# Modulations between the quarters of a panel's own weights, the norm's weight in column factors, and layer 1's transposes and gate rows inside its attention

## The chip, the cores and the metric

One Trainium2 chip, one core. The metric is the device time of one execution in microseconds; the shown value is the median of several runs. The trace comes from one more execution under the profiler.

## What is computed

A two-layer block and then one layer of a second block, all float32, 256 tokens of 2048 columns. Cut to what matters here:

```python
# first block; adaLN vectors come from one row c times a wide matrix
for l in range(2):
    mod = silu(c) @ w_mod[l] + b_mod[l]              # 2048 x 6144
    shift, scale, gate = split(mod, 3)
    h = x * (1 + scale) + shift
    y = diff_attention(h, ...) if l == 0 else forgetting_attention(h, w_q, w_out, k, v, F)
    # layer 1: k, v, F from shared_kv(x, silu(c) @ w_mod_kv + b_mod_kv, ...)
    x = layer_norm(sqrt(2) * x + gate * y, ln_g[l], ln_b[l])
# forgetting attention: o = softmax(q k' + F[t] - F[s]) v * silu(g);  return o @ w_out
# second block: S5 mixer, GLU, squared-relu MLP, with its own modulation (2048 x 12288)
```

Between the layers stands `x = layer_norm(...)` (weight `ln_g[0]`, bias `ln_b[0]`), which feeds three things: layer 1's `h` (modulated), the keys' and values' `h` (modulated by another vector) and the residual.

## The kernel before, in words

All five engines have a program written out by hand, in one order each; two planners (`tables`, a ring of six 1 MB slots for weights and a set of PSUM banks) only count who uses which slot and which bank in which turn, so the order in `tables` must be that of every engine.

The front's matrices are taken in 24 **steps** (`FRONT`): four panels of 512 columns each of layer 0's output projection (steps 0 to 3), layer 1's q (4 to 7), g (8 to 11), k (12 to 15), v (16 to 19) and its output projection (20 to 23). A panel's weights come in four quarters of 1 MB, each a slot of the ring. float32 products are made of three products of split operands: ScalarE makes the high part of each half quarter (`w_hi`), VectorE the low part (`w_lo`), and TensorE (`multiply`) runs 96 products of 512 columns, or 192 of 256, over eight half quarters. ScalarE's `w_hi(h)` waits until half h-4 has been multiplied.

A **modulation** is 512 columns of one of the wide matrices, 4 MB, also four quarters of the ring. There are 56 (`MODS`): 20 to 27 give layer 1's shift and scale, 28 to 35 those of keys and values, 36 to 39 layer 1's gate, 40 and on the second block's. TensorE multiplies one into bank 4 (`mod`: 16 products 128x32 by 512 columns, four side by side in four column groups of the array), ScalarE copies the bank to `ROWS`, and TensorE sums four row groups into columns (`sums`, which waits for that copy). `sums(j-1)` is called at the head of `mod(j)`. Twelve modulations (`DVE_MOD`) are multiplied by VectorE, in pieces between its splits (`mod_piece`), and their quarters come in the ring between those of two panels (`DVE_PART`).

Where TensorE's modulations stand before: 23 to 25 inside layer 0's attention (`MOD_AT_A`, at t = 5, 9, 13 of 21), 26 to 28 after steps 0 to 2, 29 while the layer norm is made (`MOD_AT_LN`), 30 to 37 after steps 4 to 11 (`MOD_AT_STEP`), 41 to 46 inside layer 1's attention (`MOD_AT_B`, t = 2, 7, ..., 27 of 35). VectorE's 38, 39, 40 stand in steps 12 to 17. Each is loaded as a whole, behind the panel that it follows. SP issues the loads, in the order of the ring, and blocks at a slot until what it holds has been used.

Layer 0's attention (lines 2440 to 2469 of TensorE's program) is a loop of 21 turns over 16 score blocks, software-pipelined: scores, VectorE's bias and maximum, ScalarE's exponentials, VectorE's mix, transpose, product with v. Before it, SP reloads the projections from DRAM (`proj_d`, lines 686 to 697): q and k, then v behind the last block's end, then the gate; POOL writes the S5 state to DRAM (line 879), and VectorE and ScalarE start the attention when it has landed, since they use its buffer.

After step 3 comes `layer_norm(0)`: statistics, then for each of two row tiles (x - mean) * weight and * rstd + bias, each in two halves; TensorE transposes the result (`turn_in`), and ScalarE and VectorE apply the modulation's factor and shift per column and split it (`split_in`). The same x is transposed again before step 12, and POOL stores it in DRAM.

Layer 1's attention (lines 2504 to 2532) is the same kind of loop, 35 turns over 32 blocks of 128 or 256 columns. Behind it stand `to_T(1)`, the transposes of the attended heads with their split, the broadcast of the gate over the partitions (`bcast("m1g")`, into the place of half of q) and the first splits of step 20's weights.

Of the kernel before, what the change touches and what calls it, by code (L numbers as in the profile page):

```python
# [117 lines left out]
def tables():  # L118
# [12 lines left out]
    def step(n):  # L131
        for q in range(4):
            if (n, q) in DVE_PART:
                ring.use(("mod", *DVE_PART[n, q]), slots)
            ring.use(("step", n, q), slots)
        for b in range(2):
            bank.use(("step", n, b), GD)

# [44 lines left out]
    for t in range(21):  # L183
# [6 lines left out]
        if t in MOD_AT_A:  # L190
            mod(MOD_AT_A[t])
        if t >= 17:
            bank.use(("bc", "m0g", t - 17), GC)
    for layer in range(2):
        for k in range(8):
            bank.use(("oT", layer, k), (GO, GA)[layer])
        if layer:
            for q in range(4):
                bank.use(("bc", "m1g", q), GC)
        for n in (range(0, N_W1), range(N_W1, N_GLU))[layer]:  # L200
# [6 lines left out]
            if n in MOD_AT_STEP:  # L207
                mod(MOD_AT_STEP[n])
# [7 lines left out]
        for t in range(35):  # L216
# [6 lines left out]
            if t in MOD_AT_B:  # L223
                mod(MOD_AT_B[t])
    bank.use(("ss", 1), GC)
# [24 lines left out]
def build(nc, A, out):  # L250
    ctx = ExitStack()
    with ctx:
# [8 lines left out]
                 "pcol", "xn", "xres", "xsq", "ysq", "ones", "dtaken", "dmod"]  # L261
# [84 lines left out]
        def chunk_lo(*key):  # L346
# [15 lines left out]
                ("mpost", A["norm_mlp_post_2"].rearrange("l (r n) -> (l r) n", n=128), 16)]  # L362
# [33 lines left out]
        def mod_acc(j):  # L396
            at = MSB if j > 47 else L2
            return at[:, 512 * (DVE_NO[j] % 2):512 * (DVE_NO[j] % 2) + 512]
# [89 lines left out]
        bcA, lnG, lnB = reg(24576, 2048), reg(26624, 2048), MSB[:, :]  # L488
        res_tmp = sm[:, 0:512]
# [145 lines left out]
        def sync_program(sp):  # L635
# [18 lines left out]
            def load_w(key, W, k0, n0):  # L654
                for q in range(4):
# [3 lines left out]
                    load(key, W, k0, n0, q)  # L659

# [36 lines left out]
            sp.dma_start(reg(4096, 4096), proj_d[3]).then_inc(S["p3"], 16)  # L697
# [3 lines left out]
            for t in sorted(MOD_AT_A):  # L701
                mod(MOD_AT_A[t])

# [13 lines left out]
            for n in range(N_W1):  # L717
                step(n)
                if n in MOD_AT_STEP:
                    mod(MOD_AT_STEP[n])  # L720
# [67 lines left out]
        def gpsimd_program(g):  # L788
# [94 lines left out]
            def norm_rows(l):  # L883
# [4 lines left out]
                g.dma_start(lnG, A["ln_g"][l:l + 1, :].to_broadcast([128, 2048])).then_inc(S["bcg"], 16)  # L888
# [17 lines left out]
        def scalar_program(a):  # L906
# [37 lines left out]
            def to_T(layer):  # L944

                for k2 in range(8):
# [238 lines left out]
            for t in range(21):  # L1185
# [16 lines left out]
                if t in MOD_AT_A:  # L1202
                    mod(MOD_AT_A[t])
# [7 lines left out]
            for n in range(N_W1):  # L1211
                if n == N_Q:
# [3 lines left out]
                    split_in("q", h_raw["q"], sc1, M("m1", 0), 2, AHk, 8 * n)  # L1216
# [131 lines left out]
        def vector_program(v):  # L1348
# [76 lines left out]
            def round_of(n, last=False):  # L1425
                for h in range(8 * n + 4, 8 * n + (8 if last else 12)):
# [6 lines left out]
                    w_lo(h)  # L1433
                    if n < 8 and h % 2:
# [3 lines left out]
                if last:  # L1438
                    finish(n)

# [497 lines left out]
            def layer_norm(l):  # L1938
# [7 lines left out]
                v.wait_ge(S["bcg"], 16 * (l + 1))  # L1946
                v.wait_ge(S["bcb"], 16 * (l + 1))
# [9 lines left out]
            for n in range(N_W1):  # L1957
                if n == N_Q - 1:
                    mod_bias("m1s")
                if n == N_Q:  # L1960
                    layer_norm(0)
                    own()
                    ts(sc1, M("m1", 16), 1.0, None, ADD, None, *o.up("scol"))
                    split_in("q", h_raw["q"], sc1, M("m1", 0), AHk, ALk, N_Q, 8 * n)
# [679 lines left out]
```

## Time and profile before

| | us |
|---|---|
| median of 3 runs | 2741.72 |
| lowest and highest | 2737.67, 2751.97 |
| profiled execution, its own time | 2757.5 |
| its span | 2755.6 |

Busy of the span: TensorE's products 2501.9 (91%), its weight loads 2059.6, VectorE 1714.8 (62%), ScalarE 1041.8 (38%), GpSimd 177.4. TensorE's granted clock was 0.925 of 2.4 GHz on average: it has two levels, 1.2 and 2.4 GHz, so 0.50 in a stretch is the lower and 1.00 the higher. The DMA engines read 646.77 MB.

How to read it: times in rows are from the span's start. A row of a timeline names the engine, the line, the operation, what is written and read, and in brackets the idle time before it with what ended it. "x8" are eight records; a float32 product leaves two.

### The profile page before, as it was taken

The page shows a single profiled execution, that of the slowest core. Times are in us where ns is not written, and L with a number is a line of the kernel's source. Part 1 is how long each engine was busy: PE and PEld are TensorE (multiplying, and loading weights), DVE is VectorE, ACT ScalarE, POOL GpSimd, SP SyncE. Part 2 cuts the span into 40 slices and gives each one's busy share as a digit, 9 for nine tenths or more (in the row PEclk, how much of TensorE's full clock was granted, in tenths as well). Part 3 has the DMA queues.
Part 4 walks back from the last instruction along what each step waited for, and adds up shares of the span by engine and source line. Part 5 has one row for each costly group of instructions (what it writes and reads, how often), then busy time and mean ns, then how long its engine had stood idle before and what let it go on. Part 6 is the DMA issues. An engine that isn't in the chain of part 4 may idle for free.

```text
span 2755.6 us, 42740 instructions
## 1 busy us (share of the span) xinstructions
PE 2501.9 (91%) x18111; PEld 2059.6 (75%) x18111; DVE 1714.8 (62%) x2630; ACT 1041.8 (38%) x1556; POOL 177.4 (6%) x289
## 2 busy tenths in 40 slices
PE   5799999798789799989998958899899999999998
PEld 1588877566656598789854848578699898998986
DVE  4657789688767755356524755777755477655555
ACT  0253343344453333344423322344444444343443
POOL 1102233011100000111000000000000000000000
PEclk7799999899899899989977975999999999999999
DMA  9969999787678688969766748868645587755553
GB/s 353 337 219 356 349 336 313 234 294 288 244 260 308 244 286 308 353 209 312 258 220 218 249 90 309 327 232 276 236 133 189 183 274 276 244 184 191 188 171 107
DMA packets 317373, 699.74 MB, mean 254 GB/s; under 512 B 13600, under 2 KB 14080, under 8 KB 312192
## 3 DMA queue, kind: packets, MB, share of 16 engines
q1 hardware_dynamic: 298432, 627.27, 66.2%
q0 software_dynamic: 18480, 67.66, 7.0%
q8 instruction: 143, 2.34, 0.3%
q10 hardware_dynamic: 272, 2.10, 0.2%
q14 instruction: 46, 0.38, 0.0%
HBM read 646.77 MB, written 56.49 MB: 255 GB/s over the span
## 4 chain that ended last, share of the span: by engine, by line
PE 73%; DVE 15%; DMA 8%; ACT 2%; issue 1%; SPq 0%; POOL 0%; DVEq 0%; ACTq 0%; POOLq 0%
PE bank L2147 71%; DVE arena L1352 5%; DMA ring<-in_w_mod 3%; DMA ring<-in_a_w_in 3%; DVE ring_lo L1352 3%; DVE sm L1352 2%; DVE arena L1360 2%; PE bank L2150 1%; PE bank L2375 1%; DMA ring<-in_a_w_out 1%; DMA arena<-arena 0%; DVE MSB L1352 0%; DMA m_state<-MSB 0%; DVE LT L1360 0%; ACT att_w_hi L963 0%
## 5 line engine op out<-in xcount | busy, mean ns | idle before, releaser
L1352 DVE TENSOR_TENSOR ring_lo<-ring,w_hi 128x1024 fp32r<-128x1024 f32 (+1 forms) x380 | 427.7, 1134 | 359.9 <-ACT w_hi L963 334.8
L963 ACT CAST w_hi<-ring 128x1024 fp32r<-128x1024 f32 x316 | 330.6, 1049 | 472.5 <-PE bank L2147 470.4
L1352 DVE TENSOR_TENSOR ring_lo<-ring,att_w_hi 128x1024 fp32r<-128x1024 f32 x192 | 232.0, 1223 | 224.1 <-ACT att_w_hi L963 223.9
L963 ACT CAST att_w_hi<-ring 128x1024 fp32r<-128x1024 f32 x192 | 198.9, 1049 | 350.8 <-PE bank L2147 181.0
L2147 PE MATMUL bank<-in_hi,w_hi 128*128 128x256 f32 x1024 | 290.2, 283 | 1.2 <-DVE n L1357 1.2
L2147 PE MATMUL bank<-in_lo,w_hi 128*128 128x256 f32 x1024 | 290.1, 283 | 0.0
L2147 PE MATMUL bank<-in_hi,ring_lo 128*128 128x256 f32 x1024 | 289.7, 283 | 0.0
L2147 PE MATMUL bank<-w_hi,hid_lo 128*128 128x512 f32 x640 | 257.5, 402 | 5.2 <-DVE ring_lo L1352 5.2
L2147 PE MATMUL bank<-ring,cpad 128*32 128x512 f32 x1408 | 195.7, 691 | 26.1 <-DMA ring<-in_w_mod 22.5
L2147 PE MATMUL bank<-att_w_hi,att_hi 128*128 128x512 f32 x512 | 206.0, 402 | 6.9 <-DVE ring_lo L1352 6.9
L2147 PE MATMUL bank<-ring_lo,att_hi 128*128 128x512 f32 x512 | 202.7, 396 | 0.0
L2147 PE MATMUL bank<-w_hi,hid_hi 128*128 128x512 f32 x512 | 202.6, 396 | 0.0
L2147 PE MATMUL bank<-att_w_hi,att_lo 128*128 128x512 f32 x512 | 202.0, 395 | 0.0
L2147 PE MATMUL bank<-ring_lo,hid_hi 128*128 128x512 f32 x512 | 201.5, 394 | 0.0
L913 ACT CAST in_lo<-ring 128x512 fp32r<-128x512 f32 x192 | 115.6, 623 | 213.9 <-PE bank L2147 107.7
L2147 PEld LDWEIGHTS bank<-in_hi,w_hi 128*128 128x128 f32 x1024 | 195.2, 191 | 1.4 <-DVE n L1357 1.3
L2147 PEld LDWEIGHTS bank<-in_hi,ring_lo 128*128 128x128 f32 x1024 | 194.9, 190 | 0.0
L2147 PEld LDWEIGHTS bank<-in_lo,w_hi 128*128 128x128 f32 x1024 | 194.4, 190 | 0.1
L1352 DVE TENSOR_TENSOR ring_lo<-ring,in_lo 128x512 fp32r<-128x512 f32 x192 | 129.5, 702 | 72.2 <-ACT in_lo L913 72.2
L2147 PE MATMUL bank<-hid_lo,in_lo 128*128 128x256 f32 (+1 forms) x528 | 156.1, 296 | 16.2 <-DVE ring_lo L1352 16.2
L2147 PE MATMUL bank<-w_hi,in_hi 128*128 128x512 f32 x368 | 148.6, 404 | 3.3 <-DVE ring_lo L1352 3.3
L2147 PE MATMUL bank<-att_hi,att_w_hi 128*128 128x256 f32 x512 | 146.6, 286 | 2.3 <-issue 2.3
(259 smaller groups left out, 4998.5 us busy)
## 6 DMA issues: line engine op xcount, KB each, us to landing
ring<-in_w_mod SPq DMA_DIRECT2D x192, 1024.0 KB, 9.5
ring<-in_a_w_in SPq DMA_DIRECT2D x64, 1024.0 KB, 10.2
ring<-in_w_mlp_in SPq DMA_DIRECT2D x64, 1024.0 KB, 5.2
ring<-in_w_mlp_out SPq DMA_DIRECT2D x64, 1024.0 KB, 5.1
ring<-in_kv_w_mod SPq DMA_DIRECT2D x32, 1024.0 KB, 10.7
ring<-in_b_w_in SPq DMA_DIRECT2D x32, 1024.0 KB, 6.9
ring<-in_kv_w SPq DMA_DIRECT2D x32, 1024.0 KB, 5.6
ring<-in_s_w_glu SPq DMA_DIRECT2D x32, 1024.0 KB, 5.5
```

Of the source, the lines that this page charges most:

```text
L913: return a.copy(dst, src).then_inc(*(to or o.up("act")))
L963: a.copy(whi(h), raw_half(h)).then_inc(*o.up("whi"))
L1352: return v.tensor_tensor(dst, x, y, op).then_inc(*(to or o.up("dve")))
L1360: return v.scalar_tensor_tensor(out=dst, in0=x, scalar=s1, in1=y, op0=o1, op1=o2).then_inc(*(to or o.up("dve")))
L2147: return p.matmul(dst, l_, r_, start=start, stop=stop, skip_group_check=True)
L2150: return p.transpose(dst, src, ident[0:k, 0:k])
L2375: t = p.transpose(bank("u", run, pc)[:, 32 * j:32 * j + 32], HT[run][at, e, j, :, :].rearrange("p q h -> p (q h)"), ident[at, at])
```

## The change

It keeps the work of modulations and moves it: 23 to 26 go into steps 0 to 3 and 29 to 36 into steps 4 to 11, with each quarter loaded and multiplied behind two half quarters of the panel; 27 and 28 stand at the layer norm; none stands in layer 0's attention; 37 goes to VectorE (steps 12 and 13), with 38 to 40 two steps later each, and the last quarter of 40 in the first turns of layer 1's attention. `sums(j-1)` of these modulations is called at the head of `multiply`. The load of the gate projection (proj 3) is issued behind the wait for the S5 state. `layer_norm(0)` makes only (x - mean) * rstd; the modulation's factor and shift take in the norm's weight and bias as columns, and x itself is given its weight and bias in 16 pieces in steps 4 and 5. In layer 1's attention the modulations stand at t = 5, 10, ..., 30, seven of eight transposes at t = 8, 12, ..., 32, the gate's broadcast at t = 18, 22, 26, 30 and the first splits of step 20 at t = 31 to 34.

```diff
-MOD_AT_A = {5: 23, 9: 24, 13: 25}
-MOD_AT_STEP = {0: 26, 1: 27, 2: 28, **{n: 26 + n for n in range(4, 12)}}
-MOD_AT_LN = (29,)
-MOD_AT_B = {2 + 5 * i: 41 + i for i in range(6)}
+MOD_AT_STEP = {**{n: 23 + n for n in range(4)}, **{n: 25 + n for n in range(4, 12)}}
+MOD_AT_LN = (27, 28)
+MOD_AT_B = {5 + 5 * i: 41 + i for i in range(6)}
+TURN_AT_B = {4 * k + 8: k for k in range(7)}
+GATE_AT = {18 + 4 * q: q for q in range(4)}
...
-DVE_MOD = {38: 12, 39: 14, 40: 16, 47: 20, 48: 24, 49: 26, 50: 28, 51: 30, 52: 40, 53: 42, 54: 44, 55: 46}
+DVE_MOD = {37: 12, 38: 14, 39: 16, 40: 18, 47: 20, 48: 24, 49: 26, 50: 28, 51: 30, 52: 40, 53: 42, 54: 44, 55: 46}
...
-SUMS_AT = {12: 37, 14: 38, 16: 39, 18: 40, 20: 46, 22: 47, 26: 48, 28: 49, 30: 50, 31: 51, 42: 52, 44: 53, 46: 54, 48: 55}
+SUMS_AT = {12: 36, 14: 37, 16: 38, 18: 39, 20: 46, 22: 47, 26: 48, 28: 49, 30: 50, 31: 51, 42: 52, 44: 53, 46: 54, 48: 55}
+DVE_PART[N_W1 - 1, 3] = DVE_PART.pop((N_W1, 0))
...
@@ build: vecs, the row copies
-                ("mpost", A["norm_mlp_post_2"].rearrange("l (r n) -> (l r) n", n=128), 16)]
+                ("mpost", A["norm_mlp_post_2"].rearrange("l (r n) -> (l r) n", n=128), 16),
+                ("lng", A["ln_g"][0:1].rearrange("l (r n) -> (l r) n", n=128), 16),
+                ("lnb", A["ln_b"][0:1].rearrange("l (r n) -> (l r) n", n=128), 16)]
+        lnG0 = [L2[:, 512 * i:512 * i + 512] for i in range(3)] + [L1[:, 1536:2048]]
+        q_shift = st[:, 176:192]
...
@@ sync_program, load_w
                     load(key, W, k0, n0, q)
+                    if key[0] == "step" and key[1] in MOD_AT_STEP:
+                        j = MOD_AT_STEP[key[1]]
+                        load(("mod", j), MOD_W[MODS[j][0]], 0, 128 * MODS[j][1], q)
...
             sp.wait_ge(S["blm"], 32)
-            sp.dma_start(reg(4096, 4096), proj_d[3]).then_inc(S["p3"], 16)
             sp.wait_ge(S["ms0"], 16 * 16)
             sp.wait_ge(S["ms1"], 16 * 16)
-            for t in sorted(MOD_AT_A):
-                mod(MOD_AT_A[t])
+            sp.dma_start(reg(4096, 4096), proj_d[3]).then_inc(S["p3"], 16)
             for n in range(N_W1):
                 step(n)
-                if n in MOD_AT_STEP:
-                    mod(MOD_AT_STEP[n])
...
@@ scalar_program (the same inserts stand in vector_program, with w_lo)
-                    split_in("q", h_raw["q"], sc1, M("m1", 0), 2, AHk, 8 * n)
+                    split_in("q", h_raw["q"], sc1, q_shift, 2, AHk, 8 * n)
                 if t in MOD_AT_B:
                     mod(MOD_AT_B[t])
-            for h in range(8 * N_W1, 8 * N_W1 + 4):
-                w_hi(h)
-            to_T(1)
-            bcast("m1g", bcA)
+                if t - 1 in GATE_AT:
+                    bcast("m1g", bcA, GATE_AT[t - 1])
+                if t - 1 in TURN_AT_B:
+                    to_T(1, TURN_AT_B[t - 1])
+                if t > 30:
+                    w_hi(8 * N_W1 + t - 31)
+            to_T(1, 7)
...
@@ vector_program
+                    if n in (N_Q, N_Q + 1):
+                        ln_piece(8 * (n - N_Q) + h - 8 * n - 4)
...
+            def ln_piece(i):
+                t2, c = i // 8, i // 2 % 4
+                cs = slice(512 * c, 512 * c + 512)
...
+                if i % 2 == 0:
+                    tt(xv[:, t2, cs], xv[:, t2, cs], lnG0[c], MUL)
+                else:
+                    tt(xv[:, t2, cs], xv[:, t2, cs], lnB[:, cs], ADD, *o.up("ln" if c == 3 else "dve"))
...
+                if l == 0:
+                    own()
+                    for t2 in range(2):
+                        ts(xv[:, t2, :], xv[:, t2, :], mv[:, t2, 0:1], st[:, 6 + t2:7 + t2], SUB, MUL, *o.up("xhat"))
+                    return
...
                 if n == N_Q:
                     layer_norm(0)
-                    ts(sc1, M("m1", 16), 1.0, None, ADD, None, *o.up("scol"))
+                    mod_bias("m1s")
+                    stt(sc1, M("m1", 16), 1.0, C("lng"), ADD, MUL)
+                    stt(q_shift, M("m1", 16), 1.0, C("lnb"), ADD, MUL)
+                    tt(q_shift, q_shift, M("m1", 0), ADD, *o.up("scol"))
...
+                if t < 4:
+                    mod_piece(N_W1 - 1, 4 + t)
...
@@ tensor_program
+            def mod_part(j, q):
+                w = chunk("mod", j, q)
+                p.wait_ge(*landed("mod", j, q))
+                if q == 0:
+                    room("mod", j)
+                for i in range(4):
+                    t = mm(bank("mod", j)[32 * i:32 * i + 32, :], cwide[:, 4 * q + i, :], w[:, i, :], q == 0, q == 3)
+                t.then_inc(*(fill("mod", j) if q == 3 else (S["taken"], 1)))
...
             def multiply(n):
+                if n in MOD_AT_STEP and MOD_AT_STEP[n] - 1 not in SUMS_AT.values():
+                    sums(MOD_AT_STEP[n] - 1)
...
                     if r < 7:
                         t.then_inc(S["half"], 1)
+                    if r % 2 and n in MOD_AT_STEP:
+                        mod_part(MOD_AT_STEP[n], r // 2)
...
-                if t_ in MOD_AT_A:
-                    mod(MOD_AT_A[t_])
...
-                    p.wait_ge(S["ln"], 2)
+                    p.wait_ge(S["xhat"], 2)
                     turn_in("q", xv)
                 elif n == N_K:
+                    p.wait_ge(S["ln"], 2)
                     turn_in("k", xv)
...
+                if t_ in GATE_AT:
+                    bcast("m1g", M("m1", 32), GATE_AT[t_])
+                if t_ in TURN_AT_B:
+                    k2 = TURN_AT_B[t_]
+                    p.wait_ge(*emptied("fo", 4 * k2 + 3))
+                    to_T(1, k2)
             p.wait_ge(*emptied("fo", 31))
-            to_T(1)
-            bcast("m1g", M("m1", 32))
+            to_T(1, 7)
```

## Rows read from the trace of the kernel before

**Rows 1.** The chain of waits, three of its pieces: start, duration, what it was.

```profile
736.90 11.23 DMA m_state<-MSB
...
872.58 5.04 DMA ring<-in_a_w_out
...
913.15 12.93 PE bank L2147 x54
```

**Rows 2.** Timeline of SP's queue, start of kernel and before layer 0's attention.

```profile
5.81 0.42 SPq L669 DMA_DIRECT2D arena<-in_norm_mlp_pre  x1
...
735.24 0.55 SPq L697 DMA_DIRECT2D arena<-proj  x1
```

**Rows 3.** Who waited for whom, 811 to 927: total, times, longest us.

```profile
PE bank L2147 <- DVE ring_lo L1352: 6.9, 5, 2.9
```

**Rows 4.** TensorE's timeline, at the layer norm and behind step 11.

```profile
942.63 5.44 PE L2150 MATMUL bank<-ident,arena 128*128 128x128 f32 x28 [10.82 <-DVE arena L1360]
...
1170.10 0.95 PE L2147 MATMUL bank<-sel,mod_rows 128*128 128x1 f32 x8
```

**Rows 5.** Busy by stretch: length, PE, PEld, DVE, ACT, POOL, clock, DMA, GB/s.

```profile
764.00:776.00 12.00, 11.01 (x72) 6.70 (x71) 8.19 (x28) 7.58 (x29) 0.00 (x0) 1.00 1.05 387
...
955.00:1186.00 231.00, 224.92 (x1500) 185.68 (x1500) 117.84 (x156) 86.66 (x102) 17.64 (x32) 0.97 0.87 305
...
1391.00:1520.00 129.00, 114.12 (x566) 66.57 (x567) 50.00 (x150) 40.04 (x117) 1.10 (x2) 0.76 0.64 231
```

**Rows 6.** TensorE's timeline, layer 1's attention and its tail.

```profile
1482.46 0.69 PE L2150 MATMUL bank<-ident,LT 128*128 128x128 f32 x2 [0.99 <-ACT LT L910]
...
1507.54 2.57 PE L2150 MATMUL bank<-ident,arena 128*128 128x128 f32 x12 [0.45 <-DVE arena L1360]
...
1516.65 3.56 PE L2147 MATMUL bank<-ident,MODC 128*128 128x128 f32 x30
```

**Rows 7.** VectorE's timeline, layer 0's attention, four of eight odd blocks.

```profile
749.18 0.69 DVE L1360 SCALAR_TENSOR_TENSOR LT<-LT,bank 128x512 f32<-128x512 f32 x1
...
764.20 0.69 DVE L1360 SCALAR_TENSOR_TENSOR LT<-LT,bank 128x512 f32<-128x512 f32 x1
...
768.83 0.69 DVE L1360 SCALAR_TENSOR_TENSOR LT<-LT,bank 128x512 f32<-128x512 f32 x1
...
793.83 0.69 DVE L1360 SCALAR_TENSOR_TENSOR LT<-LT,bank 128x512 f32<-128x512 f32 x1
```

**Rows 8.** TensorE's timeline, modulations: a quarter, four quarters, sums, low clock.

```profile
761.50 1.07 PE L2147 MATMUL bank<-ring,cpad 128*32 128x512 f32 x8 [1.63 <-DMA ring<-in_w_mod]
...
771.42 3.64 PE L2147 MATMUL bank<-ring,cpad 128*32 128x512 f32 x32
...
841.75 0.95 PE L2147 MATMUL bank<-sel,mod_rows 128*128 128x1 f32 x8
...
1486.88 6.47 PE L2147 MATMUL bank<-ring,cpad 128*32 128x512 f32 x32
```

**Rows 9.** TensorE's timeline, first of three such waits between 22 and 52.

```profile
27.63 1.87 PE L2147 MATMUL bank<-sel,mod_rows 128*128 128x1 f32 x8 [0.70 <-ACT mod_rows L913]
```

**Rows 10.** ScalarE's timeline behind step 5 (a q panel).

```profile
1014.60 1.08 ACT L991 ACTIVATE arena<-bank 128x512 f32<-128x512 f32 x2
1015.57 1.05 ACT L963 CAST att_w_hi<-ring 128x1024 fp32r<-128x1024 f32 x1
1016.50 0.60 ACT L913 COPY mod_rows<-bank 128x512 f32<-128x512 f32 x1
```

**Rows 11.** VectorE's timeline, layer norm and before step 12.

```profile
932.54 2.48 DVE L1360 SCALAR_TENSOR_TENSOR arena<-arena,st 128x1024 f32<-128x1024 f32 x2
...
1180.22 0.18 DVE L1356 TENSOR_SCALAR st<-MODC 128x16 f32<-128x16 f32 x1
```

**Rows 12.** Instructions of line 1357: duration ns min, median, max; when; forms.

```profile
L1357 DVE TENSOR_SCALAR arena<-arena x4: 685/688/693, 1761.1 to 1793.0; 128x1024 f32<-128x1024 f32 x4
```

**Rows 13.** VectorE's timeline in the tail of layer 1's attention.

```profile
1507.40 4.62 DVE L1352 TENSOR_TENSOR ring_lo<-ring,att_w_hi 128x1024 fp32r<-128x1024 f32 x4
```

More of the change, by code:

```diff
@@ L135, in step @@
             ring.use(("step", n, q), slots)
+            if n in MOD_AT_STEP:
+                ring.use(("mod", MOD_AT_STEP[n], q), slots)
         for b in range(2):
             bank.use(("step", n, b), GD)
+        if n in MOD_AT_STEP:
+            bank.use(("mod", MOD_AT_STEP[n]), GM)
     def tile(i):
@@ L194, in tables @@
     for layer in range(2):
-        for k in range(8):
+        for k in range(8) if layer == 0 else (7,):
             bank.use(("oT", layer, k), (GO, GA)[layer])
-        if layer:
-            for q in range(4):
-                bank.use(("bc", "m1g", q), GC)
         for n in (range(0, N_W1), range(N_W1, N_GLU))[layer]:
@@ L224, in tables @@
                 mod(MOD_AT_B[t])
+            if t in GATE_AT:
+                bank.use(("bc", "m1g", GATE_AT[t]), GC)
+            if t in TURN_AT_B:
+                bank.use(("oT", 1, TURN_AT_B[t]), GT)
     bank.use(("ss", 1), GC)
@@ L396, in mod_acc @@
         def mod_acc(j):
-            at = MSB if j > 47 else L2
-            return at[:, 512 * (DVE_NO[j] % 2):512 * (DVE_NO[j] % 2) + 512]
+            i = DVE_NO[j] % 2
+            return MSB[:, 512 * i:512 * i + 512] if j > 47 else (L2[:, 0:512], L1[:, 1536:2048])[i]
         def mod_base(j):
@@ L942, in bcast, with to_T @@
                     copy(dst[:, 512 * q:512 * q + 512], bank("bc", which, q)[:, :], *empty("bc", which, q))
-            def to_T(layer):
-                for k2 in range(8):
+            def to_T(layer, *part):
+                for k2 in part or range(8):
                     a.wait_ge(*filled("oT", layer, k2))
@@ L1945, in layer_norm @@
                 newton(st[:, 6:8], st[:, 4:6], st[:, 8:10], 2 + l)
-                v.wait_ge(S["bcg"], 16 * (l + 1))
-                v.wait_ge(S["bcb"], 16 * (l + 1))
+                if l == 0:
+                    own()
+                    for t2 in range(2):
+                        ts(xv[:, t2, :], xv[:, t2, :], mv[:, t2, 0:1], st[:, 6 + t2:7 + t2], SUB, MUL, *o.up("xhat"))
+                    return
+                v.wait_ge(S["bcg"], 16 * 3)
+                v.wait_ge(S["bcb"], 16 * 2)
                 for t2 in range(2):
@@ L1986, in vector_program @@
                     mod_bias("kv")
-                elif n == N_K + 4:
+                elif n == N_K + 6:
                     mod_bias("m1g")
@@ L2015, in vector_program @@
                     v.tensor_reduce(s_[:, 0:1], p, AX, MAX, negate=True).then_inc(*o.up("fmax"))
-            for h in range(8 * N_W1, 8 * N_W1 + 4):
-                w_lo(h)
-            to_T(1)
+                if t < 4:
+                    mod_piece(N_W1 - 1, 4 + t)
+                if t - 1 in TURN_AT_B:
+                    to_T(1, TURN_AT_B[t - 1])
+                if t > 30:
+                    w_lo(8 * N_W1 + t - 31)
+            to_T(1, 7)
             v.tensor_reduce(of_row, ident[:, :].rearrange("p (c q) -> p q c", q=8), AX, ADD).then_inc(*o.up("dve"))
@@ L2183, in mod @@
                 for q in range(4):
-                    w = chunk("mod", j, q)
-                    p.wait_ge(*landed("mod", j, q))
-                    if q == 0:
-                        room("mod", j)
-                    for i in range(4):
-                        t = mm(bank("mod", j)[32 * i:32 * i + 32, :], cwide[:, 4 * q + i, :], w[:, i, :], q == 0, q == 3)
-                    t.then_inc(*(fill("mod", j) if q == 3 else (S["taken"], 1)))
+                    mod_part(j, q)
+            def mod_part(j, q):
[6 more added lines that the diff above has]
+                t.then_inc(*(fill("mod", j) if q == 3 else (S["taken"], 1)))
             def turn_scaled():
```

25 lines of the change are left out of this document (11 added, 14 removed).

## The prediction

> **What bounds the kernel now.** I read the stages first (busy time in stretches), then the chain of waits, then each engine's timeline inside the stages that the change touches. Over most of the span TensorE is the bound; where it is not, it waits for a transfer or for a chain of small steps. Four places matter. In layer 0's attention VectorE sets the pace, but first it waits for the last state block, which took 11.2 us to land because 4 MB of projections had been asked for just before [rows 1, 2]; and three modulations cut into its loop. In the front panels 0 to 3 TensorE is all but full; the reader is to see how little it idles there [rows 3]. Around the layer norm it waits for VectorE [rows 4]. In layer 1's attention its clock is at 1.2 GHz for about half of the stretch (0.76 granted on average) [rows 5], and all that follows the loop stands in a tail [rows 6].
>
> The sum is made against the profiled execution: 2757.5 us, 1.9 above its span, and 15.8 above the median of 2741.7. I apply the difference to the median. A measurement can tell about 0.5% (13.7 us) from no change.
>
> **The change, part by part.**
>
> *Start.* Two more row copies (norm weight and bias) stand ahead of the first modulation's load on SP: one such issue takes 0.42 [rows 2], and the loads behind are on the chain. **+0.9**.
>
> *The last state block.* proj 3 (2.1 MB) is no longer issued at 735.2 but after the state has landed. At 387 GB/s [rows 5] it is worth 5.4 us of bandwidth. The gain is 0 if the block's own latency sets the end, 5.4 if all three transfers end together, as the 11.2 us suggest [rows 1]; near the upper end: **-4** (0 to -5.4).
>
> *Attention of layer 0.* Modulations 23 to 25 leave it. The odd score blocks' VectorE additions stand at 749.18 and, seven pairs later, at 793.83; a pair without a modulation takes 4.63 (764.20 to 768.83) [rows 7]. 44.65 - 7 x 4.63 = 12.2, all of it gone: **-12.2**. What is late next is VectorE itself, which has no idle time in such a pair. The panel weights now stand first in the ring and have landed long before they are used.
>
> *Panels 0 to 3.* They take four modulations in place of three. One costs 3.64 for its products and 0.95 for the sums [rows 8], 4.5 as they overlap: **+4.5**. The idle times behind late weights add up to 6.9, of which 2.9 stands in panel 0 behind the transposes and stays [rows 3]; the interleaved order frees two slots every 6.5 us and needs 5.4 us to refill them, so the rest goes: **-4.0** (0 to -4). x and the two norm rows (4.2 MB, 11 us) land in panel 0; three pairs of slots ahead just cover that.
>
> *A wait that is new.* multiply(n) now begins with sums(j-1), and j-1 was multiplied in the panel just before. It needs ScalarE's copy of the row. Before, a whole panel lay between. Where the kernel already does this, in the first modulations, TensorE idles 0.70 each time with ScalarE otherwise free [rows 9]. In the panels ScalarE also has the next cast in front of the copy (1.05), and for q and gate panels one more bank to empty (1.07 for two) [rows 10]. Panel ends at E; last modulation quarter until E+1.0; ScalarE: bank E+0.6, cast E+1.5, copy E+2.1; sums at E+2.2. So 0.7 after panels 0 to 2, about 1.15 after 4 to 10: 3 x 0.7 + 7 x 1.15 = **+10.2** (0 to 13). Behind this wait in TensorE's queue stands the whole next panel.
>
> *Quarters instead of blocks.* One quarter of a modulation alone takes 1.07, four together 3.64 [rows 8]. So a quarter is 0.857 and each block has 0.21 beside it, a tail that may or may not lie under what follows. Twelve modulations in four blocks each are 36 blocks more: 0 to 7.7, and I take **+7**, since the next products use the whole array and cannot start on the columns still in use. The Trainium skill (TensorEngine Tiling (Array Packing), Key Properties) says that changing the tiling mode drains TensorE; it gives no figure. By that rule all 36 tails would count, which is the upper end; a rule against this change, and the row bears it out as far as one block goes.
>
> *Layer norm.* Step 3 ends at 926.1 (a piece of the chain from 913.15 that lasts 12.93), the transposes begin at 942.6, 16.5 later [rows 1, 4]. VectorE's four pairs of passes, 2.5 a pair from 932.5 on [rows 11], become two tensor_scalar passes. One over 1024 columns took 0.69 [rows 12], so 1.3 each: normalized at +9.0. Were they as slow per column as the pass before (2.5 for a row of 2048) it would be +11.4. But TensorE must first do modulations 27 and 28, where it did one. 27 is in the ring; of 28 two quarters can be asked for at +0 and +1, two more only as 27 is used, at +3.6 and +4.5. A load lands 5.0 after its issue [rows 1], then one each 2.7 (1.05 MB at 387 GB/s [rows 5]): the last at +13.3, used at +14.2. So this transfer takes VectorE's place: **-2.3** (0 to -5). The affine part moves to 16 passes of 512 columns in steps 4 and 5; 16 x 0.69 = 11 us at the rate of the additions of that size [rows 7]. VectorE was busy for 117.8 of 231 us in these eight steps [rows 5], so it has room: nothing, and 11 if that cover were gone.
>
> *Into panel 12.* Step 11 ended at 1170.1, but the first casts of step 12 had to be waited for, and the factor was made at 1180.2 [rows 4, 11]. Now they are made inside step 11 and the factor comes at about +2.9; against that modulation 36 stands inside step 11 (4.5) and no longer under this wait: 7.3 - 4.5, less the table load on ScalarE: **-2.4**.
>
> *Panels 12 to 19.* One modulation more on VectorE, which has room: nothing.
>
> *Layer 1's attention.* In the tail TensorE went from 1507.5 to 1520.2 through transposes and broadcast, with four cast passes of VectorE (4.6) under it [rows 6, 13]; only one transpose pair remains: -12.2. In the loop, TensorE idles 0.99 per pair at full clock [rows 6], and VectorE longer. Four transposes (0.86 at 1.2 GHz: 12 took 2.57) and a broadcast quarter (0.89 at full clock) just fit there; at 1.2 GHz there is hardly room. I count 0.4 for each of 7 transposes, 0.5 more for three at low clock, 1.5 for two of four broadcasts, 2.5 for the cast passes in the emptying loop, 1.0 for the last part of modulation 40 and 1.9 for its sums: 11.2. **-1** (between -12.2 with all hidden and +6 if each costs its full low-clock time).
>
> **Sum**: 0.9 - 4 - 12.2 + 4.5 - 4.0 + 10.2 + 7 - 2.3 - 2.4 - 1 = -3.3, so 2754.2 for a profiled execution and **2738.4** for the median.
>
> **Rivals.**
> *The clock falls in layer 0's attention (slower).* The three bursts of modulation are gone from a loop that is otherwise no denser than the one of layer 1. With them the granted clock was 1.00, in layer 1's attention 0.76 [rows 5]. At 1.2 GHz TensorE's share of a pair (11.0 busy less 3.6 for the modulation, over 1.9 pairs: 3.9) becomes 7.8 and passes VectorE's 4.63: +3.1 for up to 7 pairs, 22 us; it decides from the point where the clock is low for more than one pair. Less idle in the measure of busy time gives 15 to 18 as more likely: 2738.4 + 18 = 2756. For it: layer 1's loop. Against: this loop has 256-column products where that one has 128. The Trainium skill (TensorE: Matmul & The Clock Gate, What's actually happening) says "the default state is throttled, and activity releases the throttle", which speaks the same way. Chance 0.1.
> *The clock holds in layer 1's attention (faster).* Transposes and broadcasts fill it. A modulation at 1.2 GHz took 6.5 against 3.6 [rows 8]; four spared, with their sums, are some 12 us: 2726. Chance 0.15.
> *Row copy and block tails cost little (faster).* If ScalarE is earlier than I think, or tails overlap, two thirds of the 17 us go: 2727. Chance 0.12.
> *The interleaved loads are late after all (no gain in steps 0 to 3).* x, norm rows and ring collide in step 1, the 4.0 stays and 3 to 6 are added: 2746. Chance 0.1.
> *My sum*, within 2729 to 2748: 0.53.
>
> **Numbers.** Under 2728.0: 0.02 of my own case, 0.13 of the second rival, 0.1 of the third: 0.25. Over 2755.4: 0.07 of the first, 0.02 of the last, 0.02 of mine: 0.11. The rest, 0.64, is within 0.5%. The range 2722 to 2754 takes in the faster rivals and most of the bounds (the block tails at 0, the attention at +6) and leaves out the clock's fall.
>
> **What would show it.** Right: pairs of 4.6 at clock 1.00 in layer 0's attention; an idle of about 0.7 or 1.2 before each sums, released by ScalarE's row copy; TensorE's last wait before the norm's transposes named a load of the ring. Wrong: a granted clock of 0.50 in layer 0's loop, no idle before the sums, panels with a modulation no longer than before, or TensorE waiting for VectorE's splits in steps 4 and 5.

## The result, and the profile after

The changed kernel takes **2774.3 us** (median of 4 runs, 2769.4 to 2779.6) against 2742.4 (4 runs, 2737.7 to 2752.0): a ratio of **1.0112 [1.0078, 1.0147]**, 32 us slower. Measured again it was 2776.0 against 2748.3, 1.0097 [1.0076, 1.0119]. I had forecast 2738.4 with a range to 2754: wrong.

The profiled execution took 2771.6 (span 2769.8), only 14.2 of span more than that of before, since that one was 15.8 over its median; 9.6 of those lie ahead of all that was changed (the last block of state transposes began at 728.5 before and at 718.9 after; in later profiles, of either kind, it began between 718.3 and 724.2). From there on the two profiles are 23.8 apart. Page of the changed kernel, busy line and two groups of matmuls:

```profile
PE 2516.7 (91%) x18079; PEld 2058.0 (74%) x18079; DVE 1732.4 (63%) x2658; ACT 1040.9 (38%) x1555; POOL 175.8 (6%) x290
...
L2185 PE MATMUL bank<-ring,cpad 128*32 128x512 f32 x1376 | 197.6, 691 | 25.7 <-DMA ring<-in_w_mod 19.6
L2185 PE MATMUL bank<-att_w_hi,att_hi 128*128 128x512 f32 x512 | 212.8, 416 | 4.3 <-DVE ring_lo L1365 2.9
```

TensorE has one modulation less than before (x1376 where x1408 stood; VectorE took it), and yet it is busy for 14.8 us longer: the first hint of a clock. Stage by stage, both profiles read at the same instructions:

| stage | before | after | difference | my terms |
|---|---|---|---|---|
| last state block to first transposes (layer 0's attention) | 80.7 | 65.2 | -15.6 | -16.2 |
| first transposes to end of panel 3 | 117.8 | 128.0 | +10.2 | +4.9 |
| end of panel 3 to panel 4 (layer norm) | 28.3 | 26.3 | -2.0 | -2.3 |
| panel 4 to the forget gate's product | 234.1 | 259.1 | +25.0 | +10.4 |
| to layer 1's attention | 201.9 | 203.1 | +1.2 | 0 |
| layer 1's attention, to panel 20 | 128.8 | 130.4 | +1.6 | -1 |
| the rest, to the last product | 1222.8 | 1226.3 | +3.4 | 0 |

A stage's length is a difference of start times; the last column has what my sum put into it. Two stages hold the miss, both with modulations in quarters. First, who TensorE waited for from 955 to 1187 in the changed kernel (total, times, longest in us):

```profile
PE bank L2185 <- ACT mod_rows L924: 9.5, 7, 2.3
```

That wait I had (7 x 1.15 = 8.1). ScalarE's timeline at the end of panel 5 shows it as forecast: bank, cast, row copy, one behind the other, and the sums at the end of them [rows 10]:

```profile
998.22 1.11 ACT L1002 ACTIVATE arena<-bank 128x512 f32<-128x512 f32 x2
999.22 1.03 ACT L974 CAST att_w_hi<-ring 128x1024 fp32r<-128x1024 f32 x1
1000.15 0.59 ACT L924 COPY mod_rows<-bank 128x512 f32<-128x512 f32 x1
```

The longest of the seven, in front of panel 9, has one thing more ahead of the copy, which my 1.15 left out: panel 8 is the first g panel, and ScalarE first loads another function table (its timeline, then TensorE's):

```profile
1090.04 1.28 ACT L921 ACT_TABLE_LOAD   x1
1091.34 1.08 ACT L921 ACTIVATE MSB<-bank 128x512 f32<-128x512 f32 x2
1092.31 1.05 ACT L974 CAST att_w_hi<-ring 128x1024 fp32r<-128x1024 f32 x1
```

```profile
1093.89 1.87 PE L2185 MATMUL bank<-sel,mod_rows 128*128 128x1 f32 x8 [2.34 <-ACT mod_rows L924]
```

What I had not at all is what stands behind the sums. TensorE's timeline at the end of panel 5 again:

```profile
1000.79 1.13 PE L2185 MATMUL bank<-sel,mod_rows 128*128 128x1 f32 x8 [1.11 <-ACT mod_rows L924]
...
1002.36 0.41 PE L2185 MATMUL bank<-att_hi,ring_lo 128*128 128x256 f32 x1
1002.57 0.41 PE L2185 MATMUL bank<-att_hi,att_w_hi 128*128 128x256 f32 x1
...
1004.70 0.41 PE L2185 MATMUL bank<-att_lo,att_w_hi 128*128 128x256 f32 x1
...
1005.22 0.28 PE L2185 MATMUL bank<-att_lo,att_w_hi 128*128 128x256 f32 x1
1005.34 0.28 PE L2185 MATMUL bank<-att_hi,ring_lo 128*128 128x256 f32 x1
```

From 1002.1 to 1004.9 the starts are 0.21 apart, from 1005.1 on 0.12: for some 3 us TensorE runs at 1.2 GHz, and then at 2.4 again. The granted clock says the same, for panels 5 to 7 and in two short stretches (length, PE, PEld, DVE, ACT, POOL, clock, DMA share, GB/s):

```profile
968.34:999.68 31.34, 30.09 (x232) 26.12 (x232) 21.70 (x34) 9.90 (x12) 0.00 (x0) 0.95 0.78 268
999.68:1030.90 31.22, 30.11 (x232) 26.14 (x232) 17.25 (x26) 9.41 (x12) 0.54 (x1) 0.95 0.95 337
1030.90:1060.79 29.89, 28.58 (x232) 24.62 (x232) 16.37 (x25) 10.02 (x12) 0.00 (x0) 1.00 0.81 282
...
1001.00:1005.00 4.00, 4.00 (x23) 4.00 (x23) 2.81 (x6) 0.00 (x0) 0.54 (x1) 0.58 1.05 393
1033.00:1036.00 3.00, 3.00 (x27) 3.00 (x27) 1.58 (x4) 0.00 (x0) 0.00 (x0) 1.00 1.05 401
```

Six of the seven waits in front of sums are followed by such a stretch (7 to 16 slow products, 10.3 us together); panel 7, in the third row, is spared and is 1.3 to 1.5 shorter. Behind the wait of 2.34 the low clock begins with the sums (1.87 for them, 1.05 in front of panels 2 and 3) and lasts almost 7 us. In the kernel before, the clock was 1.00 from 966 to 1170, panels with their modulations included (the 0.97 of [rows 5] takes in the slow start of panel 4 and what follows panel 11), and a q panel took 27.4.

### The profile page after: what moved, and what is told of

It reads as the page before. It is cut to its first block, busy times and chain, and to the rows that moved or that the text cites. A ratio compares the mean times of both kernels' runs of the same rounds, so it can differ in the third digit from the quotient of the medians.

```text
span 2769.8 us, 42717 instructions
## 1 busy us (share of the span) xinstructions
PE 2516.7 (91%) x18079; PEld 2058.0 (74%) x18079; DVE 1732.4 (63%) x2658; ACT 1040.9 (38%) x1555; POOL 175.8 (6%) x290
## 3 DMA queue, kind: packets, MB, share of 16 engines
q8 instruction: 143, 2.34, 0.3%
## 4 chain that ended last, share of the span: by engine, by line
PE 71%; DVE 14%; DMA 9%; ACT 3%; issue 2%; SPq 0%; POOL 0%; DVEq 0%; ACTq 0%; POOLq 0%
PE bank L2185 69%; DVE arena L1365 5%; DMA ring<-in_a_w_in 3%; DMA ring<-in_w_mod 2%; DVE ring_lo L1365 2%; DVE sm L1365 2%; DMA ring<-in_b_w_in 1%; DVE arena L1373 1%; PE bank L2188 1%; PE bank L2420 1%; ACT att_w_hi L974 1%; DVE LT L1373 1%; DMA arena<-arena 0%; DVE MSB L1365 0%; DVE st L1948 0%
## 5 line engine op out<-in xcount | busy, mean ns | idle before, releaser
L2185 PE MATMUL bank<-ring,cpad 128*32 128x512 f32 x1376 | 197.6, 691 | 25.7 <-DMA ring<-in_w_mod 19.6
L2185 PE MATMUL bank<-att_w_hi,att_hi 128*128 128x512 f32 x512 | 212.8, 416 | 4.3 <-DVE ring_lo L1365 2.9
```

Of the source, the lines that this page charges most:

```text
L2185: return p.matmul(dst, l_, r_, start=start, stop=stop, skip_group_check=True)
```

## The experiments

All comparisons are with the kernel before on the same chip; its median was 2743.7 to 2748.3 in them.

**The sums away from the panel's head.**

```diff
-                if n in MOD_AT_STEP and MOD_AT_STEP[n] - 1 not in SUMS_AT.values():
-                    sums(MOD_AT_STEP[n] - 1)
...
+                    if r == 1 and n in MOD_AT_STEP and MOD_AT_STEP[n] - 1 not in SUMS_AT.values():
+                        sums(MOD_AT_STEP[n] - 1)
                     if r % 2 and n in MOD_AT_STEP:
```

> The changed kernel, with each sums(j-1) moved from the head of the panel to behind its second weight block, ahead of the first modulation quarter. By then ScalarE's copy of the row is long done. Theory A (the wait for the row copy, and after it some 3 us in which TensorE's granted clock is 0.50 to 0.63, seven times in panels 5 to 11): idle 9.5 us and 6 x 1.6 us of slow products go, and 3 x 0.7 us in front; 2774 - 20 = 2754 us. Theory B (the quarters between the blocks are what costs, the slow clock comes from them): only the idle goes, and the clock still dips in every panel; 2774 - 11 = 2763 us. In its trace A wants no idle time released by mod_rows in panels 5 to 11 and a granted clock of 1.00 in each of them.

Measured: 2743.0, ratio 0.9986 [0.9972, 1.0000]. So where two lines stand makes the whole loss, 31 us. Theory A's direction held, its size (20) was too small: it left out the longer wait and the slow products behind panel 0, and layer 1's attention too was 4.2 shorter in this profile. No wait for the row copy is left in these panels, and the granted clock is 1.00 (same columns):

```profile
970.60:999.01 28.41, 28.41 (x234) 24.64 (x233) 21.71 (x33) 9.85 (x11) 0.54 (x1) 1.00 0.86 282
1083.51:1111.36 27.85, 27.85 (x137) 19.42 (x136) 10.71 (x11) 9.71 (x11) 4.38 (x8) 1.00 0.95 339
```

By stage, panels 4 to 11 with the turn went from 259.1 to 237.4 and the front panels from 128.0 to 119.6: 30 us.

**Modulations whole again**, behind each panel, in panels 0 to 11 (one addition of VectorE's moves from behind panel 10 to behind panel 11, since its sums come later):

```diff
-            if n in MOD_AT_STEP:
-                ring.use(("mod", MOD_AT_STEP[n], q), slots)
...
             step(n)
+            if n in MOD_AT_STEP:
+                mod(MOD_AT_STEP[n])
...
-                    if r % 2 and n in MOD_AT_STEP:
-                        mod_part(MOD_AT_STEP[n], r // 2)
```

> The changed kernel with the modulations of panels 0 to 3 and 4 to 11 back in one piece behind each panel, weights and all; which modulation stands where, the layer norm and both attentions stay as changed. Theory A (row-copy wait, slow clock after it, and 0.3 us for each of 36 extra blocks): 20 us as in the run before and another 11 us go, late loads give 4 back; 2774 - 27 = 2747 us, panels with a modulation back at 27.4 us from 31.1. Theory C (the interleaving is not the cause: the slower time comes from the layer norm's extra modulation, the last state block's order or layer 1's attention): within 8 us of the changed kernel, 2766 us or more.

Measured: 2740.4, ratio 0.9975 [0.9960, 0.9990]. Panels 5 and 6 are back at 27.43, and Theory C is out. With the run before it gives the price of a block: 28.41 - 27.43 = 0.98 for three extra ones, **0.33 each**. Of the expected 11 us only 3 show in the time, for the whole modulations give some back elsewhere: a modulation is no longer inside panel 3 and stands at the layer norm as a third (35.3 from the end of panel 3 to panel 4, against 26.3), and one stands in front of panel 12 (19.8 from the end of panel 11 to the gate's product, against 12.1).

**Only the quarters**, in the kernel before: its own modulations of panels 0 to 2 and 4 to 11, interleaved as in the change, nothing else.

```diff
             ring.use(("step", n, q), slots)
+            if n in MOD_AT_STEP:
+                ring.use(("mod", MOD_AT_STEP[n], q), slots)
...
+                if n in MOD_AT_STEP and MOD_AT_STEP[n] - 1 not in SUMS_AT.values():
+                    sums(MOD_AT_STEP[n] - 1)
...
+                    if r % 2 and n in MOD_AT_STEP:
+                        mod_part(MOD_AT_STEP[n], r // 2)
```

> The kernel before with only the interleaving added: the modulations of panels 0 to 2 and 4 to 11 in quarters between the panel's own blocks, with the sums of the one before at the head; nothing else changed. Theory A: 9.5 + 10 us of waits and slow clock in panels 5 to 11, 2 x 0.7 us in front, 33 extra blocks x 0.3 us = 10 us, less up to 4 us for late loads: 2742 + 27 = 2769 us. Theory C: less than 8 us over the kernel before, 2750 us or less.

Measured: 2782.1, ratio 1.0119 [1.0097, 1.0141], 35 slower. This part alone makes the whole loss. That the other parts together gain does not follow from the two medians, whose intervals overlap; it is read from the stages, where the first and the layer norm are 15.6 and 2.0 shorter in the changed kernel. Panel 4 to the gate's product took 262.2, with 10.9 us of waits in front of seven sums, and slow products behind six of them.

**A shorter wait.** The sums stay at the head, ScalarE copies the row before the last cast:

```diff
                     if h == 8 * n + 11:
                         finish(n)
+                        if n in MOD_AT_STEP:
+                            mod(MOD_AT_STEP[n])
...
                     w_hi(h)
```

> The changed kernel, with the sums still at the head of the panel, but ScalarE copies the modulation's row before the last weight cast of the round instead of behind it. The wait in front of the sums in panels 5 to 11 then shrinks from 1.1 to 1.3 us to about 0.7, and a wait of 0.7 in the front panels was followed by no slow clock. Theory A1 (what costs is the slow clock that follows a wait over 1 us, 1.6 us or more each time; a short wait is free of it): idle 7 x 0.45 = 3 us and 7 x 1.6 = 11 us go, and the run with the sums moved (2743) stays some 17 us better only by the remaining waits: 2774 - 14 = 2760 us. Theory A2 (the clock falls at the panel's head for another reason, a wait of any length will do): 2774 - 3 = 2771 us, with the clock of panels 5 to 11 still 0.90 to 0.95.

Measured: 2758.5, ratio 1.0049 [1.0033, 1.0065]: Theory A1, to 2 us. A panel is 29.29 = 28.41 + 0.7 of wait and 0.2 at its ends. Of the seven waits in front of panels 5 to 11 only one stayed long, the one with the table load, and only behind that one did the clock fall. TensorE's timeline, and the windows of two panels (length, PE, clock, DMA share, GB/s):

```profile
1025.42 0.27 PE L2187 MATMUL bank<-sel,mod_rows 128*128 128x1 f32 x1 [0.70 <-ACT mod_rows L924]
...
1084.37 0.27 PE L2187 MATMUL bank<-sel,mod_rows 128*128 128x1 f32 x1 [1.51 <-ACT mod_rows L924]
```

```profile
1025.42:1054.72 29.30, 28.59 (x233) 1.00 0.83 287
1085.97:1114.76 28.79, 28.09 (x128) 0.95 0.86 302
```

**The wait filled.** The strictest one: the sums can't start earlier than in the changed kernel, but TensorE works in the wait. The waits for the panel's two banks move ahead of the sums with it.

```diff
+                for j in range(2):
+                    room("step", n, j)
+                if n in range(1, 4) or n in range(5, 12):
+                    p.wait_ge(S["wlo"], 8 * n + 1)
+                    for _ in range(10 if kind in TURNED else 5):
+                        if kind in TURNED:
+                            mm(step_banks(n)[0][:, 0:256], whi(8 * n)[:, 0, 0:128], a_hi[:, 0, :], True, True)
+                        else:
+                            mm(step_banks(n)[0], a_hi[:, 0, 0:128], whi(8 * n)[:, 0, :], True, True)
                 if n in MOD_AT_STEP and MOD_AT_STEP[n] - 1 not in SUMS_AT.values():
                     sums(MOD_AT_STEP[n] - 1)
-                for j in range(2):
-                    room("step", n, j)
```

> The changed kernel with the wait in front of the sums left as it is, but TensorE kept busy in it: at the head of panels 1 to 3 and 5 to 11 it makes ten products of 256 columns (or five of 512, 1.07 us either way) whose result the panel's first real product overwrites. No time for the row copy is saved: the sums can't start earlier than before. Theory A1 (half of the price is the slow clock that follows TensorE's idle time): idle of 1.1 to 1.3 us turns into 0.1 to 0.2, the clock of panels 5 to 11 reads 1.00, and six stretches of slow products go, 1.6 us each: 2774 - 10 = 2764 us. Theory A2 (the clock falls whatever TensorE does there, for instance for the modulation's narrow products or the full DMA): 2774 us, or more by what the filler outlasts the wait (front panels: 3 x 0.4 us), with the clock of the panels still 0.91 to 0.95.

Measured: **2765.3**, ratio 1.0066 [1.0044, 1.0088], where the changed kernel had 2776.0 on the same chip:

> The changed kernel itself, once more, as the measure for the run with the filled wait: both theories want 2774 us, 1.1% over the kernel before.

More work, 11 us less time. The windows of panels 5 to 7 (length, PE, clock, DMA share, GB/s) no longer fall below 1.00 while the same transfers run, which leaves Theory A2 nothing:

```profile
970.00:1001.00 31.00, 31.00 (x256) 1.00 0.82 283
1001.00:1032.00 31.00, 31.00 (x254) 1.00 0.95 343
1032.00:1062.00 30.00, 30.00 (x241) 1.00 0.84 283
```

The head of a panel is no shorter for it: from the start of the last quarter's last product to the panel's own first product pass 2.6 to 2.8 us in front of panels 5 to 8 in both kernels. But these panels now last 29.7 from sums to sums, as only the spared panel 7 did in the changed kernel, where its neighbours took 31.2 and 31.4.

So the price of one such wait is shown in its two halves: about 1.2 idle, and about as much again, and somewhat more, in slow products behind it.

**Halves instead of quarters**, to test the price of a block: with the sums moved, two quarters of a modulation together behind blocks 3 and 7.

```diff
-                    if r % 2 and n in MOD_AT_STEP:
-                        mod_part(MOD_AT_STEP[n], r // 2)
+                    if r % 4 == 3 and n in MOD_AT_STEP:
+                        mod_part(MOD_AT_STEP[n], r // 2 - 1)
+                        mod_part(MOD_AT_STEP[n], r // 2)
```

> The changed kernel with the sums moved, and each modulation of panels 0 to 11 multiplied in two pairs of quarters (behind blocks 3 and 7) instead of four single ones; the loads keep their order. The trace of the run with single quarters gives 28.41 us for a panel against 27.43 with the modulation whole: 0.33 us for each of three extra blocks. Theory A: two of the three go, 12 panels x 2 x 0.33 = 7.9 us, panels of 27.76; 2743 - 8 = 2735 us. Rival: what makes the panel longer is not the number of blocks (late loads or casts instead): panels stay at 28.2 or more, 2741 us or more, since slots of the ring come free later.

Measured: 2742.5, ratio 1.0004 [0.9989, 1.0018]: no gain, and yet panels of 27.87 and 27.24 where single quarters had 28.41 and 27.85, 0.27 to 0.30 per block saved. What took it back stands at the layer norm: end of panel 3 to panel 4 went from 26.3 to 32.2, with the waits for the loads of modulation 28. Theory A is right of the block and wrong of the time. The profiles show two things in these 6 us: with halves, three quarters of modulation 28 wait for their loads (1.60, 0.94 and 0.78), where two did (0.82 and 1.66) in the run with the sums moved; and from 916.5 to 924 the granted clock is 0.52, so that a quarter takes 1.94 and not 1.06. How much belongs to each I have not separated.

**Quarters in the front panels alone**, whole modulations in panels 4 to 11, sums moved:

```diff
+MOD_BY_QUARTER = range(4)
...
-                    if r % 2 and n in MOD_AT_STEP:
+                    if r % 2 and n in MOD_BY_QUARTER:
                         mod_part(MOD_AT_STEP[n], r // 2)
...
                 multiply(n)
...
+                if n in MOD_AT_STEP and n not in MOD_BY_QUARTER:
+                    mod(MOD_AT_STEP[n])
```

> The changed kernel with the sums moved, quarters kept in panels 0 to 3 alone, and panels 4 to 11 with whole modulations behind them. It takes the better of two profiles by stage: 145.9 us from the first transposes to panel 4 (with all modulations whole: 149.2) and 235.8 us from panel 4 to the forget gate's product (with quarters: 237.4). If these stages add up: 2743 - 1.6 = 2741 us, and no slower than the 2740.4 us of the run with all modulations whole. If the extra blocks cost what the trace says (0.33 us each, 24 of them) and the waits that they cover do not come back, it is up to 8 us better than the run with quarters everywhere: 2735 us.

Measured: **2738.7**, ratio 0.9976 [0.9959, 0.9992]. With the run of whole modulations the best of all, by less than the intervals tell them apart. The stages did add up (146.0 and 235.0); the 8 us did not come.

The same with halves in front:

```diff
-                    if r % 2 and n in MOD_BY_QUARTER:
-                        mod_part(MOD_AT_STEP[n], r // 2)
+                    if r % 4 == 3 and n in MOD_BY_QUARTER:
+                        mod_part(MOD_AT_STEP[n], r // 2 - 1)
+                        mod_part(MOD_AT_STEP[n], r // 2)
```

> The run with quarters in panels 0 to 3 alone (2738.7 us), with pairs of quarters in those four panels. Theory A: 4 panels x 2 x 0.33 = 2.6 us less: 2736 us; this would be the best of all by little. Rival (loads late because slots come free later): 2739 us or more, the idle time at late weights in the front panels back to 3 us or more.

Measured: 2743.5, ratio 1.0003 [0.9990, 1.0015], for the same reason as the other run with halves (31.4 at the norm).

**Layer 1's attention undone.** With the sums moved: transposes, gate broadcasts and first casts back in the tail.

```diff
-TURN_AT_B = {4 * k + 8: k for k in range(7)}
-GATE_AT = {18 + 4 * q: q for q in range(4)}
+TURN_AT_B = {}
+GATE_AT = {}
```

> The changed kernel with the sums moved behind the second block (2743 us) and layer 1's attention undone: its seven early transposes, the gate broadcasts in the loop and the first casts all stand in the tail again, as in the kernel before; modulations 41 to 46 keep their new places. If that part of the change is worth the 12.2 us of tail less what it adds to the loop, as I had it (1 us net) or as the stages of two profiles read (126 against 129 us), this gives 2744 to 2746 us; if the loop hides the moved work better than that, up to 2753; if the filled loop costs more than the tail saves, under 2742 us.

Measured: 2744.5, ratio 0.9994 [0.9976, 1.0012], against 0.9986 with that part in: worth 1.5 us at most, and no difference that can be measured. In the profiles this stage took 126.3 without and 126.2 with it.

**The last state block first.** The kernel before, with one load issued later:

```diff
-            sp.dma_start(reg(4096, 4096), proj_d[3]).then_inc(S["p3"], 16)
 
             sp.wait_ge(S["ms0"], 16 * 16)
             sp.wait_ge(S["ms1"], 16 * 16)
+            sp.dma_start(reg(4096, 4096), proj_d[3]).then_inc(S["p3"], 16)
```

> The kernel before with one edit: the 2.1 MB load of the projections' last part is issued on SP after the waits for the last state block instead of ahead of them. My term was 4 us (0 to 5.4): 2743 us against 2747, layer 0's attention stage 77 us from 80.7 in its profile. Rival: the state block's own latency sets the end, so the stage stays at 80.7 us and the time within 1 us of before; then the whole gain of 16 us in that stage belongs to the three modulations that left it.

Measured: 2748.1, ratio 1.0006 [0.9986, 1.0027]. Both expectations missed: VectorE's wait for the block did shrink, from 14.88 to 11.27, by the 3.6 I had counted (first the kernel before, then this one),

```profile
748.20 0.42 DVE L1360 SCALAR_TENSOR_TENSOR LT<-LT,bank 128x256 f32<-128x256 f32 x1 [14.88 <-DMA m_state<-MSB]
```

```profile
739.74 0.42 DVE L1360 SCALAR_TENSOR_TENSOR LT<-LT,bank 128x256 f32<-128x256 f32 x1 [11.27 <-DMA m_state<-MSB]
```

but the stage grew to 84.4. TensorE's timeline says where it went: the first modulation of the loop now waits longer for its weights (5.6 over its four quarters, where it was 2.5), and in these waits the granted clock is 0.54 (750.0 to 760.4), so that a quarter takes 1.94 where it took 1.07. The first two quarters:

```profile
750.30 1.41 PE L2147 MATMUL bank<-ring,cpad 128*32 128x512 f32 x8 [2.69 <-DMA ring<-in_w_mod]
753.01 1.94 PE L2147 MATMUL bank<-ring,cpad 128*32 128x512 f32 x8 [1.30 <-DMA ring<-in_w_mod]
```

In the changed kernel that modulation is gone from the loop, VectorE's wait is 11.38, and the gain is kept.

## Why the prediction was wrong, step by step

**The step that failed** is *A wait that is new*: "0.7 after panels 0 to 2, about 1.15 after 4 to 10: 3 x 0.7 + 7 x 1.15 = +10.2". The mechanism, its place and its releaser were right and the idle time nearly so (9.5 from panel 4 on, where I had 8.1). The price of a wait was not: I put it at its idle time. The clock of TensorE falls to 1.2 GHz behind it, for some 3 us (almost 7 behind the longest), at another 1.5 to 2.1 us of slow products each. The two runs that leave the order as it is, with the wait shortened (2774 to 2758) and with the wait filled (2776 to 2765), show this; the one that removes the wait gives 31 us. I had looked for a falling clock in both attentions and priced it there; in the panels I read 0.97 [rows 5] and took it as given, though the clock was granted to a TensorE without one pause in them. The highest of my cases was 2756.

The rest of the front panels' excess is the same wait in panel 0, where I had 0.7. There ScalarE first waits for a load and then makes two casts ahead of the row copy:

```profile
822.44 1.99 ACT L974 CAST att_w_hi<-ring 128x1024 fp32r<-128x1024 f32 x2 [7.00 <-DMA ring<-in_a_w_out]
824.34 0.58 ACT L924 COPY mod_rows<-bank 128x512 f32<-128x512 f32 x1
```

Timeline of TensorE in the changed kernel: the sums behind panel 0, at low clock, and behind panel 1.

```profile
824.97 1.87 PE L2185 MATMUL bank<-sel,mod_rows 128*128 128x1 f32 x8 [2.83 <-ACT mod_rows L924]
...
856.52 1.05 PE L2185 MATMUL bank<-sel,mod_rows 128*128 128x1 f32 x8 [0.71 <-ACT mod_rows L924]
```

So the rival of late loads had a true piece: the load was asked for at 803, x and the norm rows at 805 to 806, and from 800 to 824 the DMA share is 1.02 to 1.04: they do collide in panel 0. Panels 2 and 3 waited 0.7 each as forecast, at full clock.

*Quarters instead of blocks*: right in kind, too small. I took 7 us, with 0.21 a block as the upper end (7.7 in all); in place a block costs 0.33 in a q panel, and 36 of them at that price 11.9. The 0.21 was a record's length beyond its work. The starts show what it misses:

```profile
1008.79 0.28 PE L2185 MATMUL bank<-att_lo,att_w_hi 128*128 128x256 f32 x1
1008.91 0.28 PE L2185 MATMUL bank<-att_hi,ring_lo 128*128 128x256 f32 x1
1009.12 1.06 PE L2185 MATMUL bank<-ring,cpad 128*32 128x512 f32 x8
1010.11 0.38 PE L2185 MATMUL bank<-att_hi,att_w_hi 128*128 128x256 f32 x1
1010.34 0.28 PE L2185 MATMUL bank<-att_lo,att_w_hi 128*128 128x256 f32 x1
```

The last product in front is followed after 0.21 and not 0.12, the quarter takes 0.99, and the first product behind is followed after 0.23: 1.19, where a quarter's work is 0.857. The Trainium skill (TensorEngine Tiling (Array Packing), Key Properties) says that a change of tiling mode drains TensorE; by that rule both sides of a block pay, and the trace agrees: I had counted one side.

These two terms, with the longer waits, make 10.3 (slow products from panel 5 on) + 0.8 (slow sums in front of panel 9) + about 3 (slow products and sums behind panel 0) + 1.4 and 2.1 (waits) + 4.9 (blocks) = 22.5, where the two stages exceed my terms by 20. The step into panel 12, 0.6 better than forecast, is part of the second; the rest of the difference I can't place.

*Attention of layer 0* and *the last state block*: right together, 15.6 of 16.2, with VectorE's pairs at 4.64. The clock was not the 1.00 that I named as a sign, but 0.93 from 736 to 784; the pairs did not grow by it, so the rival in which the clock falls for many pairs did not happen. The block's 4 us are real, but only because the modulations left: the parts were not independent, as the run with the load alone shows.

*Layer norm*: right. The last wait ahead of the transposes is for modulation 28's last quarter, 13.8 after the end of panel 3 where I had 14.2:

```profile
925.91 1.07 PE L2185 MATMUL bank<-ring,cpad 128*32 128x512 f32 x8 [1.65 <-DMA ring<-in_kv_w_mod]
```

*Idle time of the front panels*: gone as forecast, the only wait left for casts is the 2.9 in panel 0. *Into panel 12*: 19.6 became 12.1, which with the 4.5 moved away is -3.0, where I had -2.4. *Layer 1's attention*: -1 forecast. The changed kernel's profile has +1.6 and that with the sums moved -2.7; the clock moves this stage by more than the change does: among the profiles that have it, it took 130.5 at a granted clock of 0.80 and 122.4 to 122.6 at 0.85 or 0.86. Why the clock differs is open. Panel 20 gives 1.4 back: it now starts behind a nearly idle tail, at 1.2 GHz (23.9 from its first product to the first sums, 22.5 in the run with the tail undone). The *start* term of 0.9 is below what profiles tell apart.

## What to carry to other kernels

A short wait at the head of a dense stretch of TensorE can cost more than its idle time: here waits of 1.1 us and more were mostly followed by slow products worth as much again or more, and waits of 0.7 by none. So put a small step that depends on another engine's last work behind the first blocks of the new stretch, not ahead of them. Splitting work of another shape into dense products costs at both edges of each block; read that from the distances between starts, not from the lengths of records. A part that is worth its price in the whole change can be worth nothing alone, as the later load of proj 3 was.

## What the runs showed of the hardware

- Waits of TensorE of 1.1 to 2.6 us between a modulation's last quarter and the sums in front of panels 5 to 11 were followed by 1.2 GHz in 18 of 21 cases (the changed kernel twice, and the kernel before with quarters): behind the 14 of up to 1.3 us for some 3 us, beginning 0.8 to 1.9 after the start of the sums; behind the four of 2.3 to 2.6 for almost 7 us, beginning with the sums. It followed none of the waits of 0.7 us, in the run with the shorter wait or in front of panels 2 and 3. The three exceptions (1.31, 1.11 and 1.23 us) are all in front of the same panel, 7. With the wait filled, three that stayed (1.42, 1.49 and 0.95, in front of panels 1, 9 and 10) were followed by no slow product: length alone does not decide, and what else does is open.
- Ten useless products of 256 columns (or five of 512) in front of each of ten panels made the kernel 11 us faster. The Trainium skill (TensorE: Matmul & The Clock Gate, A second HAM failure mode: psum-queue depth-cycling) tells of short idle times of TensorE between groups of products that make its clock go back and forth; the trace shows the same, though here with only one pause in 30 us.
- A block of four products of 32 columns' width between full ones costs 0.33 us beyond its work (a q panel with three such blocks more takes 28.41 in place of 27.43).
